# Summing the later convolutions in PSUM, giving GpSimd the gates' subtractions, and moving the turning of q and k in a three-layer network kernel

## What is computed

```python
h = rmsnorm(x, norm1_g[l])
u = h @ w_in[l]                      # q, k, v (512 each), glu_in (1024), four_in (512)
q = apply_partial_rope(rmsnorm(q, qnorm_g[l]), cos, sin)      # groups of 32
k = apply_partial_rope(rmsnorm(k, knorm_g[l]), cos, sin)
# 8 heads, two components c of 32: w = softmax(q0 k0) - lam * softmax(q1 k1); out = w @ v
y_a = (rmsnorm(att, subln_g[l]) * (1.0 - lam_init)) @ w_proj_a[l]
g = ga * jax.nn.sigmoid(gb)
cv = depthwise_conv(g, conv_w[l], width 31)   # 512 channels
y_b = jax.nn.silu(layernorm(cv + conv_b[l])) @ w_proj_b[l]
y_c = real(fft2(four_in))  @ w_proj_c[l]
gates = jax.nn.sigmoid(h @ w_gate[l] + b_gate[l])             # 3 x 1024
x = x + (gates0 * y_a + gates1 * y_b + gates2 * y_c) @ w_out[l]
h2 = rmsnorm(x, norm2_g[l])
x = x + (silu(h2 @ w_gate_half) * (h2 @ w_up_half)) @ w_ffn_out[l]   # inner width 2816
```

## Time and profile before

| | us |
|---|---|
| median of 3 runs | 1431.55 (1429.74 to 1433.89) |
| the profiled execution | 1431.48 |
| its span | 1430.2 |

### The profile page before, as it was taken

One profiled execution on the slowest core, in us unless ns is written; L12 is line 12 of the kernel. 1 busy time (PEld: TensorE's weight loads), 2 busy tenths in 40 slices (PEclk: granted clock), 3 DMA queues, 4 the chain that ended last, 5 costly groups with the idle time before them and its releaser, 6 DMA issues. The chain is left out here.

```text
span 1430.2 us, 21050 instructions
## 1 busy us (share of the span) xinstructions
PE 1347.8 (94%) x8946; PEld 1218.7 (85%) x8946; DVE 902.4 (63%) x1173; ACT 656.4 (46%) x902; POOL 164.7 (12%) x118
## 2 busy tenths in 40 slices
PE   7999999989998898899998999999889999899999
PEld 6878889889986796678997999879667899799987
DVE  5655465568774559976576555445997657655543
ACT  5634435355553453344644444344334564444432
POOL 0100030113330005200110000000620011000000
PEclk9999999999998999999999999999999999999999
DMA  8643234444554454223344555556322334355551
GB/s 333 220 183 131 89 104 177 176 154 171 177 177 167 158 209 148 88 89 118 126 170 162 179 187 190 181 176 210 147 89 88 118 133 162 148 183 189 189 178 58
DMA packets 33503, 226.49 MB, mean 158 GB/s; under 512 B 3713, under 2 KB 4097, under 8 KB 7425
## 3 DMA queue, kind: packets, MB, share of 16 engines
q1 hardware_dynamic: 33408, 225.14, 43.9%
HBM read 224.08 MB, written 1.05 MB: 157 GB/s over the span
## 5 line engine op out<-in xcount | busy, mean ns | idle before, releaser
L1474 DVE TENSOR_TENSOR wlo<-raw,whi 128x2048 fp32r<-128x2048 f32 x205 | 470.9, 2300 | 305.2 <-ACT whi L913 236.8
L509 PE MATMUL ps<-hhi,whi 128*128 128x256 f32 x1696 | 490.6, 289 | 2.9 <-DVE hlo L1507 2.2
L510 PE MATMUL ps<-hlo,whi 128*128 128x256 f32 x1696 | 483.4, 285 | 0.0
L511 PE MATMUL ps<-hhi,wlo 128*128 128x256 f32 x1696 | 483.2, 285 | 0.0
L913 ACT ACTIVATE whi<-raw 128x2048 fp32r<-128x2048 f32 x205 | 388.7, 1900 | 166.2 <-PE ps L458 146.8
L509 PEld LDWEIGHTS ps<-hhi,whi 128*128 128x128 f32 x1696 | 329.0, 194 | 15.5 <-issue 13.9
L510 PEld LDWEIGHTS ps<-hlo,whi 128*128 128x128 f32 x1696 | 329.3, 194 | 0.4 <-issue 0.2
L511 PEld LDWEIGHTS ps<-hhi,wlo 128*128 128x128 f32 x1696 | 328.9, 194 | 0.0
L1353 POOL TENSOR_TENSOR st<-st,sm 128x1 f32<-128x1 f32 (+2 forms) x30 | 46.2, 1540 | 694.3 <-DVE st L1526 367.3
L456 PE MATMUL ps<-whi,hhi 128*128 128x512 f32 (+1 forms) x272 | 110.9, 408 | 8.2 <-DVE hlo L1507 6.3
L456 PE MATMUL ps<-whi,ghi 128*128 128x512 f32 x264 | 104.2, 395 | 7.1 <-DVE fu L1871 7.0
(11 more groups left out here) (267 smaller groups left out, 1784.4 us busy)
## 6 DMA issues: line engine op xcount, KB each, us to landing
raw<-in_w SPq DMA_DIRECT2D x203, 1024.0 KB, 4.8
gain<-in_rows SPq DMA_DIRECT2D x5, 512.0 KB, 3.7
raw<-in_w SPq DMA_DIRECT2D x8, 256.0 KB, 6.6
raw<-in_w SPq DMA_DIRECT2D x2, 560.0 KB, 8.0
x<-in_x SPq DMA_DIRECT2D x2, 512.0 KB, 5.1
csT<-in_cs SPq DMA_DIRECT2D x2, 512.0 KB, 5.6
out<-x SPq DMA_DIRECT2D x2, 512.0 KB, 2.8
dec<-in_dec SPq DMA_DIRECT2D x1, 768.0 KB, 6.8
```

What stands on the lines that cost most here:

```text
L509: pe.op.matmul(o, wh[:, k, c:c + 128], hi[:, k, :], start=first, stop=False, skip_group_check=True)
L510: pe.op.matmul(o, wh[:, k, c:c + 128], lo[:, k, :], start=False, stop=False, skip_group_check=True)
L511: ins = pe.op.matmul(o, wl[:, k, c:c + 128], hi[:, k, :], start=False, stop=last, skip_group_check=True)
L1474: dve.op.tensor_tensor(t.wlo[i % NHL][:, c], t.raw[i % NRAW][:, c], t.whi[i % NHL][:, c].bitcast(F32), ALU.subtract).then_inc(*at("dve_lo" ...
```

## The change

- POOL_LO: the lower halves of the gates' chunks, all but the first in each layer (11 a layer), are made by GpSimd in four pieces of 128x512 (`split`), after q's and k's rotations; VectorE skips them.
- The convolution sums in PSUM bank 3, two channel blocks at a time, each in half of the bank; the last tap writes to `t.cv`. The ring has three banks from the end of v to the end of attention (`keep`, `give_back`). Its taps are spread otherwise: 1 a step in k's and q's loops, 2 in xf's, 4 a Fourier step, 4 or 5 a half-head.
- Of the two exponentials the second stays in its PSUM bank; `combine` reads it there. The next scores for that bank wait for W instead of the exponentials.
- xf is projected before k is turned; q is turned inside the last Fourier step. xf has a place of its own in SBUF, so its copies wait for nothing else.
- The down products have banks 4 to 7 for themselves.
- In the first block VectorE adds yb to the merged sum instead of GpSimd. The output products (all three) wait for pairs of blocks instead of fours.

```diff
+POOL_LO = {i for l in range(2) for f in GATES[1:] for i in UNITS[f"g{l}_{f}"]}
@@ pe_program
-        data = lambda k, tt: ("mixed", u, k // 4)
+        data = lambda k, tt: ("mixed", u, k // 2 * 2)
-                banks[tt, hf] = take_bank((f"dn{n}", tt, hf))
+                banks[tt, hf] = 4 + 2 * tt + hf
+                pb.fix((f"dn{n}", tt, hf), banks[tt, hf])
@@ layer
         ev.name("pe_weights", ("v ends", l, "pe"))
+        pb.keep(("conv", l), 3)
-        qk_turned("k")
         run(rows(f"xf{l}", *h))
-        qk_turned("q")
+        qk_turned("k")
@@ fourier
+                if g == 4:
+                    qk_turned("q")
@@ attention
-                    pe.wait_ge(*on("E2", l, u - 2) if u >= 2 else on("T12", l, 2 + u))
+                    pe.wait_ge(*on("W2", l, u - 2) if u >= 2 else on("T12", l, 2 + u))
@@ after the weave
+        pb.give_back(3)
@@ act_program
-                        act.op.activation(t.E2[u % 2][:, c, :], t.sc[u % 2][:, c * S:c * S + S], ACT.Exp,
-                                          bias=nm[:, hd, tt, c:c + 1], accum_out=lw[:, hd, tt, c:c + 1]).then_inc(
+                        s = t.sc[u % 2][:, c * S:c * S + S]
+                        act.op.activation(s if c else t.E2[u % 2][:, :], s, ACT.Exp, bias=nm[:, hd, tt, c:c + 1],
+                                          accum_out=lw[:, hd, tt, c:c + 1]).then_inc(
@@ pool_program
+    def split(i):
+        pool.wait_ge(*on("raw", i))
+        pool.wait_ge(*on("hi", i))
+        pool.wait_ge(*on("used", i - NHL))
+        for k in range(4):
+            pool.op.tensor_tensor(t.wlo[i % NHL][:, half(k)], t.raw[i % NRAW][:, half(k)],
+                                  t.whi[i % NHL][:, half(k)].bitcast(F32), ALU.subtract).then_inc(
+                *at("pool_lo", *([("lo", i)] if k == 3 else [])))
@@ layer, after the rotations
+        for i in sorted(POOL_LO & set(range(UNITS[f"v{l}"][0], UNITS[f"out{l}_0"][0]))):
+            split(i)
@@ dve_program, splits
+            if i in POOL_LO:
+                continue
@@ yb_out
+            m = t.mg[0][:, 2 * f:2 * f + 2, :]
+            await_own("dve_out")
+            dve.op.tensor_tensor(m, m, t.gm[4 + f], ALU.add).then_inc(*at("dve_small", ("merged", "mo", 2 * f)))
@@ conv_some
-        todo = [(f, j) for j in range(31) for f in range(4)]
+        todo = [(f, j) for p in (0, 2) for j in range(31) for f in (p, p + 1)]
+                acc = t.pb[3][:, (f % 2) * S:(f % 2) * S + S]
-                    ins = dve.op.scalar_tensor_tensor(t.cv[:, f, :], t.gp[:, f, j:j + S], cw[:, f, j:j + 1],
-                                                      t.cv[:, f, :], ALU.mult, ALU.add)
+                    ins = dve.op.scalar_tensor_tensor(t.cv[:, f, :] if j == 30 else acc, t.gp[:, f, j:j + S],
+                                                      cw[:, f, j:j + 1], acc, ALU.mult, ALU.add)
@@ combine
-            dve.op.scalar_tensor_tensor(t.W2[u % 2][:, :], t.E2[u % 2][:, 1, :], cc[:, hd, tt:tt + 1],
-                                        t.E2[u % 2][:, 0, :], ALU.mult, ALU.add).then_inc(*at("dve_out", ("W2", l, u)))
+            dve.op.scalar_tensor_tensor(t.W2[u % 2][:, :], t.sc[u % 2][:, S:2 * S], cc[:, hd, tt:tt + 1],
+                                        t.E2[u % 2][:, :], ALU.mult, ALU.add).then_inc(*at("dve_out", ("W2", l, u)))
```

More of the change, by code:

```diff
@@ L163, in __init__, with fix, keep, give_back @@
     def __init__(self, known):
-        self.known, self.turn, self.of, self.holds = known, 0, {}, [None] * 4
+        self.known, self.ring, self.of, self.holds = known, [0, 1, 2, 3], {}, [None] * 8
     def take(self, name):
-        b = self.turn % 4
-        self.turn += 1
+        b = self.ring.pop(0)
+        self.ring.append(b)
+        return b, self.fix(name, b)
+    def fix(self, name, b):
         before, self.holds[b], self.of[name] = self.holds[b], name, b
-        return b, before
+        return before
+    def keep(self, name, b):
+        self.ring.remove(b)
+        self.of[name], self.holds[b] = self.holds[b], name
+    def give_back(self, b):
+        self.ring.append(b)
     def find(self, name):
@@ L341, in place @@
     t.sq = at("sq", y + 4, [128, 512])
-    t.xf = [at(f"xf{i}", y + 6 + 2 * i, [128, 512]) for i in range(2)]
+    t.xf = [at(f"xf{i}", p + 32 + 2 * i, [128, 512]) for i in range(2)]
     t.T12 = [at(f"T12{i}", y + 10 + 2 * i, [128, 512]) for i in range(2)]
@@ L345, in place @@
     t.cdT = at("cdT", y + 18, [128, 2, 128])
-    t.E2 = [at(f"E2{i}", y + 2 * i, [128, 2, S]) for i in range(2)]
+    t.E2 = [at(f"E2{i}", y + 2 * i, [128, S]) for i in range(2)]
     t.W2 = [at(f"W2{i}", y + 4 + i, [128, S]) for i in range(2)]
@@ L751, in down @@
             if kg == 0:
-                banks[tt, hf] = take_bank((f"dn{n}", tt, hf))
+                banks[tt, hf] = 4 + 2 * tt + hf
+                pb.fix((f"dn{n}", tt, hf), banks[tt, hf])
             ends = list(ends) + ([("got", f"dn{n}", tt, hf)] if kg == NFT - 1 else [])
-            mul3(t.pb[banks[tt, hf]][:, :], t.ghi[:, kg, tok(tt)], t.glo[:, kg, tok(tt)], wh[:, k, half(hf)],
+            mul3(t.ps[banks[tt, hf]][:, :], t.ghi[:, kg, tok(tt)], t.glo[:, kg, tok(tt)], wh[:, k, half(hf)],
                  wl[:, k, half(hf)], kg == 0, kg == NFT - 1, ends)
@@ L787, in qk_turned @@
                 turned((w, l, "T", tt), [(w, l, "roped", tt)], t.qn[n][:, :], 4)
+        run(rows(f"xf{l}", *h))
         qk_turned("k")
-        run(rows(f"xf{l}", *h))
-        qk_turned("q")
-        ev.name("pe_turned", ("projected", l, "pe"))
         def fourier():
@@ L891, in bank @@
     def bank(name):
-        return t.pb[pb.find(name)]
+        return t.ps[pb.find(name)]
     upto = [0]
@@ L1246, in layer @@
         run(rows(f"q{l}", qk_out("q")))
+        run(rows(f"xf{l}", value_out(f"xf{l}", lambda tt: t.xf[tt][:, :], [])))
         qk_turned("k")
-        run(rows(f"xf{l}", value_out(f"xf{l}", lambda tt: t.xf[tt][:, :],
-                                     [("k", l, "T", tt) for tt in range(2)])))
-        qk_turned("q")
         done = []
@@ L1378, in pool_program @@
         power(("ret rs", k), st[:, 200 + 2 * k:202 + 2 * k], st[:, 192 + 2 * k:194 + 2 * k], ("ret var", k))
-    for f in range(4):
-        j = 2 * f
-        pool.wait_ge(*on("free", (f"yb{f}", 0)))
-        pool.wait_ge(*on("ya gated", f))
-        pool.op.tensor_tensor(t.mg[0][:, j:j + 2, :], t.mg[0][:, j:j + 2, :], t.gm[4 + f], ALU.add).then_inc(
-            *at("pool_small", ("merged", "mo", j)))
     for tt in range(2):
@@ L1820, in mixed_lower @@
         jj = slice(j, j + 2)
-        lower([("mixed", u, j // 4)] * (j % 4 == 2), t.ml[m][:, jj, :], t.mg[m][:, jj, :], t.mh[m][:, jj, :],
+        lower([("mixed", u, j)], t.ml[m][:, jj, :], t.mg[m][:, jj, :], t.mh[m][:, jj, :],
               ("mixed hi", u, j))
@@ L1968, in layer @@
             for _ in rows(f"{w}{l}", qk_out(w)):
-                conv_some(2)
-        for _ in rows(f"xf{l}", value_out(f"xf{l}", t.xf[0][:, :], [("k", l, "T", tt) for tt in range(2)])):
-            conv_some(3)
+                conv_some(1)
+        for _ in rows(f"xf{l}", value_out(f"xf{l}", t.xf[0][:, :], [])):
+            conv_some(2)
         def fourier():
@@ L2026, in after_attention @@
             conv_some(len(todo))
-            ev.name("dve_small", ("conv", l))
+            ev.name("dve_small", ("conv", l), ("free", ("conv", l)))
             o16 = t.o2[:, :, :].rearrange("p t (h d) -> p (t h) d", d=64)
```

23 lines of the change are left out of this document (14 added, 9 removed).

## The result

The changed kernel takes 1385.38 us (median of 4 runs, 1383.21 to 1387.17), the kernel before 1431.01 beside it (4 runs, 1429.74 to 1433.89): a ratio of 0.968 with an interval of 0.966 to 0.970, 45.6 us. The prediction said 1391 with 1382 to 1406.

What follows compares the result with a forecast made beforehand. TensorE, at its matmuls 94% of the span, was taken as the bound, so only its idle time and slow stretches could be won: 23.4 + 14.0 - 3.8 + 1.6 + 2.7 + 3.1 = 41.0, 1431.5 to 1390.5, said as 1391, range 1382 to 1406.

Steps and rivals of the forecast that it cites:

- Turned later: q, k turned later around xf and the Fourier part: TensorE's waits for GpSimd go, 11.7 us a layer, 23.4 in all.
- first rival: Waits move instead of going: q's bank is freed as late as before at xf, 1404, range 1398 to 1408; chance 0.17.
- The c projection's second pair: With three banks, TensorE newly waits for the first pair's bank: 1.9 us a layer lost, 3.8 in all.
- Attention: Splits leave VectorE, so TensorE's stops (6.0 us) and slow clock (1.3) go: 14.0 us for both layers.
- Taps in PSUM: Convolution taps on VectorE with their sum in PSUM take 0.42 to 0.45 us each; other end 0.68.
- second rival: Taps in PSUM are slow: at 0.9 us a tap VectorE is late in attention, about 1423; chance 0.05.
- GpSimd's splits: Eleven chunks a layer on GpSimd, pieces at 1.29 us, 5.2 a chunk, in time for TensorE: nothing lost.
- third rival: In attention GpSimd's pieces and VectorE exclude each other: 3.2 us a piece, 1492; slower from 2.5; chance 0.04.
- The smaller pieces: Gains outside the main stages: first output product 1.6 us, the layers' output products 2.7, first feed-forward 3.1.
- The first output product: VectorE's addition and waiting for pairs of blocks remove its second half's wait: 1.6 us gained.
- the layers' two: The two layers' output products no longer wait for the later blocks, 1.37 us each: 2.7 gained for two.
- The down products: First feed-forward: waits for the up products' banks go, a 4.3 us stop at the third chunk comes: 3.1 gained.

Runs made afterwards that it cites:

- Experiment seven: Kernel before with only the new order of turning (xf first, in its own place; q turned in the Fourier part), against the kernel before: 1433.91 us, ratio 1.003.
- experiment one: Changed kernel with the old order alone (k turned before xf, q before the Fourier part): 1400.91 us, ratio 0.979 to the kernel before.
- experiment two: Changed kernel with all the gates' lower halves made by VectorE again: 1411.28 us, ratio 0.986 to the kernel before.
- experiment three: Changed kernel with the convolution summed in SBUF again, its order of taps and the three banks kept: 1398.89 us, ratio 0.978 to the kernel before.
- Experiment four: Changed kernel with bank 3 given back before the c projection and the next chunk split before the feed-forward's last step: 1374.95 us, ratio 0.961 to the kernel before.
- experiment six: Changed kernel with both exponentials in SBUF, so W reads two SBUF inputs: 1384.73 us, ratio 0.969 to the kernel before.
- experiment eight: Changed kernel with each of GpSimd's pieces made twice: 1422.46 us, ratio 0.995 to the kernel before.
- experiment five: Changed kernel with the down products back in the ring's four banks: 1386.4 us, ratio 0.970 to the kernel before.

## Why the prediction was right, point by point

**The time.** 1385.4 lies in the range; it is 5.6 below the number. Of that, 3.3 us stand between the sum (1390.5) and the profiled execution (1387.17), 1.8 between that and the median, and 0.5 is the rounding up to 1391.

**Turned later: right in mechanism, 2.4 us a layer too small.** 11.7 was foretold, 14.1 came. Start to start the five places give 5.8 at k's second half, 1.8 of slow xf, 4.1 at q's second half, 1.1 in the first Fourier products and 1.1 before the last one: 14.0. The sum had 5.37 + 1.83 + 3.52 + 1.28 and 0.3 less. So it used the idle column, which begins where the matmul before is taken to end, and lost the slow turnings around each stop (0.4 and 0.6 us). And it left out what the earlier trace rows held: after the 3.52 us stop the first eight Fourier products ran slow as well, 583.90 to 588.54, 4.64 us, where after has 566.65 to 570.16, 3.51. The clock was charged behind one of the two stops only. GpSimd's times were guessed too late on top: q was to be just in time for 582, and it is 3.1 us early. That cost the sum no more than the 0.3 us that were kept back for it.

**And it didn't come from the order alone.** The prediction booked 23.4 us under the order and none under the taps and splits, adding terms as if they were independent. Experiment seven shows the order gaining nothing where VectorE keeps its load (1433.9 against 1429.6); experiment one shows it worth 15.5 on top of the rest. The two halves need one another: the order takes GpSimd's lateness away, the lighter VectorE has xf ready when TensorE arrives. The prediction had this dependence in its first rival (the bank of q freed late), with the tap count against it. It had the place wrong: what comes late is VectorE's copy of xf, not q's bank. And the taps are not all of it: with the splits alone put back, xf's bank is waited for by 1.4 us a layer (experiment two), so a bank can be freed late in the ring of three, though another one than the rival named. That the sum lies in PSUM is not needed for xf: experiment three has it in SBUF and no such wait. What fewer taps are worth without the splits moved was not run.

**The c projection's second pair: right.** -1.9 was foretold, and the second pair starts 2.78 us after the turning of the outputs where it was 0.79: 1.99. Experiment four, which gives the bank back earlier, has no such wait.

**Attention: right, 0.8 us a layer too small.** 7.0 was foretold as 6.0 of stops, 1.3 of slow clock less 0.3; 7.8 came, so the 0.3 was not left over and 0.5 more was won. VectorE's list was to take 3.6 us a half-head against 4.75; 17.8 us of idle time before 16 maxima and 9.0 before 4 more instructions make its real cover larger than the 1.15 that was named. The mechanism is tested by experiment two, which brings W's waits back (15.0 us, 10.1 before).

**Taps in PSUM: right.** 0.42 to 0.45 was taken as the pitch, with 0.68 as the other end: ten take 4.00 us, a step of 0.39, with 0.48 from start to end of one. The second rival (0.9 a tap) falls.

**GpSimd's splits: right.** 1.284 us a piece, 1.3 foretold; a share of 19%, 20% foretold; 183 splits on VectorE. The question that had no clean row, whether a VectorE instruction with one input in SBUF and one in PSUM is held up by GpSimd, has one now: 32 W between 475 and 481 ns, with GpSimd at work in 50 of 91 us around them. With the second input in SBUF they range from 476 to 1541 (experiment six), the taps go from 0.48 to 0.69 us and the pieces from 1.284 to 1.385 (experiment three). This is as the Trainium skill, "SBUF — State Buffer", states in its part on the shared port pair: VectorE with two SBUF inputs contends with a GpSimd instruction that reads SBUF, and with at most one SBUF input it does not, its two-port modes excepted. For taps and W both halves agree with rows now. The exception, which the prediction left out, matters too: the Trainium skill says in the same part that `tensor_scalar` can enter such a mode, and in after one with a single SBUF input takes 0.56 us, ending with GpSimd's rotation, where three others of the layer take 0.17 or 0.18. No view shows in which mode it ran.

```profile
557.80 0.56 DVE L2002 TENSOR_SCALAR st<-st 128x16 f32<-128x16 f32 x1
```

```profile
557.28 1.05 POOL L1430 TENSOR_TENSOR qn<-qn,st 128x512 f32<-128x512 f32 x1
```

**The third rival: its threshold was wrong.** It was to decide from 2.5 us a piece, yet at 2.67 (experiment eight) the kernel is still 7 us under before. Both of its times were too late, GpSimd's start (583; 572.3) and the last chunk (680; 673.6); some 4.5 us of each come from layer 0 starting earlier. Between them lie 100.5 us and not 97, and the slow steps behind the stops were left out. The two nearly cancel: 44 x 2.67 - 97 = 20.5 a layer for the 18.6 seen (half of 37.1). The step that failed is the other side: it set this against the gain outside attention alone (13.5 a layer). But 680 is a time of a schedule that has attention's gain in it already; the whole 20.5 (41 / 2) stood against the lateness. That gives (97 + 20.5) / 44 = 2.67, and with what was measured, 2.67 + (22.8 - 18.6) / 44 = 2.77, where 22.8 is half of 45.6. This is an estimate from one point: it takes the loss to grow by 44 us a layer for each us a piece.

**The smaller pieces.** The first output product: 1.3 for 1.6; the layers' two: 2.3 for 2.7, with 0.7 us of wait for ml left in each, about what was to be left. The down products: 2.7 us of trace for 3.1, with the foretold stop (4.3 then, 3.96 as seen, released by wlo, behind ScalarE's three upper halves). The medians of experiment five don't tell it from none. The output products were not taken apart by a run: what the pairs and what the addition on VectorE are worth is read from the two traces only.

**What was not foretold:** from layer 0's first up product to the end of layer 1's v after is 2.3 us longer, with the same instructions and the same two stops (3.3 us ahead of the stretch, 2.9 in it). What differs is how many of the matmuls behind them step slowly. Behind the first stop they are 12 of 256 columns in before and 23 in after (0.21 instead of 0.12 us), behind the second none and eight of 512 columns (0.43 instead of 0.23). This is not tied to the change: experiments two, four, five and eight leave this stretch as after has it, and their traces show 8 to 12 and none, those of one, three and six 23 to 26 and eight. The unprofiled executions of after had a granted clock of 0.989 to 0.990, the profiled one, the slowest of the four, 0.986.

## What to carry to other kernels

Sum waits start to start and with the slow steps on both sides of each, not from the idle column: that was the 2.4 us a layer that the prediction missed. When two parts of a change relieve two engines that are late for the same consumer, they don't add: price each with the other undone, because the second late partner hides under the first one's wait (here the order alone gained nothing and was worth 15.5 with the rest). An in-order engine with a quarter of its time free can still be what bounds a stage, if something it waits for stands ahead of what others wait for.

## What the runs showed of the hardware

VectorE's taps and W were held up by GpSimd's subtractions, and these by the taps, only where VectorE read two tensors from SBUF. With one of the two in PSUM W went from 476 to 1541 ns down to 475 to 481 (experiment six), and the mean tap from 0.69 to 0.48 (experiment three), the length that a tap in SBUF has with nothing in its way. GpSimd needs 1.28 us for the 128x512 subtraction; VectorE's 128x2048, four times as much, takes 2.29. A `tensor_scalar` of 128x16 with one SBUF input took 0.56 us beside a rotation of GpSimd and 0.17 else, so one SBUF input is no warrant for every operation. TensorE's slow steps after one and the same stop are not one number: behind the 3.4 us stop in v of layer 0, the ten traces have 6 to 14 matmuls of 512 columns at 0.43 instead of 0.23 us (8 in before, 13 in after), 8 x 0.2 = 1.6 us apart.
